# The delta stage in 64-token chunks on strips of the array, and streams' attention values on four strips

## The chip, the cores and the metric

The kernel runs on one core of a Trainium2 chip. The metric is the device time of one execution in microseconds. The engines are TensorE (PE in the profile), VectorE (DVE), ScalarE (ACT), GpSimd (POOL) and SyncE (SP), which here issues most of the loads.

## The reference

One layer of a hybrid streaming encoder: 1024 new tokens of one prompt, and 16 tokens each of 8 running streams (128 tokens), 1152 in all. After a norm and one combined input projection two branches run on the same tokens: attention over a band of 64-token chunks (8 heads of 64), and a gated DeltaNet (4 heads, keys and values of 128). Their outputs are merged by gates, projected, and followed by an MLP. The DeltaNet's part, per head, is this:

```python
q = l2_normalize(qb) * dk ** -0.5; k = l2_normalize(kb)     # qb, kb, vb: causal conv and silu of the projection
g = -exp(a_log) * softplus(a + dt_bias); beta = sigmoid(b)
gc = cumsum(g)                                              # within a chunk of 64 tokens (16 for a stream)
decay = tril(exp(gc[:, None] - gc[None, :]))
A = strict_tril(beta[:, None] * (k @ k.T) * decay) + I
u = solve(A, v * beta[:, None]); w = solve(A, k * (beta * exp(gc))[:, None])
def step(S, chunk):                                         # over the chunks in order
    v_new = u - w @ S
    o = (q * exp(gc)[:, None]) @ S + ((q @ k.T) * decay) @ v_new
    S = S * exp(gc[-1]) + (k * exp(gc[-1] - gc)[:, None]).T @ v_new
ob = rms_norm(o, delta_norm_w) * silu(z)
```

The prompt's state starts at zero, each stream's state is an input, and all final states are outputs.

## The kernel before, in words

The stages run one behind the other: norm, input projection, attention, delta stage, and a tail (projections, merge, MLP). Tokens lie in 9 tiles of 128; tiles 0 to 7 are the prompt, tile 8 holds the streams. Each stage has one program per engine, and engines wait for each other through semaphores.

*Input projection* (stage_in_proj, from L307). TensorE multiplies slabs of weights and tokens; VectorE and ScalarE copy the results out of PSUM. Ahead of the main loop the columns a and b of the gates are made, copied to SBUF (ab_row) and turned by 9 transposes of 8 rows into pab, which VectorE copies to env.ab at L420. Their exp, sigmoid and softplus are worked out later, in the delta stage.

*Attention* (stage_attention, from L510). The work goes in 72 steps, 8 blocks of 8 heads of a prompt tile and one stream: TensorE makes scores (scores_pair L833, scores_stream L844 and L847), VectorE adds the bias and takes the maximum (soft: L718, L721, L737), ScalarE exponentiates (L684), TensorE turns the probabilities (turn, L859) which ScalarE copies (L673), and TensorE makes the values (values_pair L878, values_stream L892). Of each stream all 8 heads stand in the 128 rows of one score tile, 16 rows a head. values_stream multiplies for each of 4 head pairs the transposed values (128 channels of the pair, 5 blocks of keys) by all 128 rows of probabilities: 20 matmuls on the full array, of whose result only a 16-column block per head is used. VectorE picks these blocks with 8 copies of 64x16 (L774). SyncE loads the caches, the relative-position bias (bias_s, 8 loads at L622) and others.

*Delta stage* (stage_delta, from L911). Its order is written out by hand in schedule(): a list of items (kind, tile, step). Every engine walks through that list and does its part of each item (has() says which engine has one), so the list is the order of each engine's queue; wait(engine, item) waits for another engine's part. Tiles are prepared two at a time ("prep": turn, norm_turn, decay, pair, inv0, inv1a to inv5b, solve), with two 64-token chunks side by side in a 128-token tile, block-diagonal, and the four heads in four matmuls of 128x128. In turn q, k and v are transposed into token rows; VectorE makes the normalised and scaled copies, which TensorE turns back in norm_turn and decay. The inverse of the triangular matrix is built over six block sizes (LEVELS 1 to 32): at each, part a multiplies by a masked matrix that GpSimd makes (L1108), ScalarE copies (L1183), part b multiplies twice, and VectorE subtracts twice (L1297, L1299), always 512 columns. Between the preps of a pair stand the "scan" items of the pair before: read (L1454, L1456), then v_new on VectorE (L1307), then write (L1462, L1465), then the state on VectorE (L1310); GpSimd makes the decayed state (L1119). At the end of the list stand the streams' heads (8 masked matmuls with 8 states, each head) and all finals (norm, gate and transposes of the outputs). At its start the stage works out the gates on ScalarE and VectorE, loads the conv output of all tokens in three loads (C, L1051) and takes the row norms of q and k through squares (L1138), pick matmuls (L1354) and transposes (L1359); the gates' z are loaded late.

## Time and profile before

| | us |
|---|---|
| median of 3 runs | 2310.87 (2308.77 to 2315.36) |
| the profiled execution | 2308.39 |
| its span | 2306.7 |
| norm | 0 to 47.3 |
| input projection | 47.3 to 617.0 |
| attention | 617.0 to 884.1 |
| delta stage | 884.1 to 1264.3 |
| tail | 1264.3 to 2306.7 |

Over the span TensorE is busy for 2117.7 us (92%) with 12384 instructions, VectorE for 888.0, ScalarE for 644.4, GpSimd for 610.4. Half of TensorE's time belongs to the input projection and the tail. A share of busy time is an average over stages with different limits; the views by stage and by stretch, the timeline and the durations of single instructions say more for a change within one stage. PEld in the profile is the loading of weights, which runs beside PE. "Clock" is the granted TensorE clock as a share of full speed.

### The profile page before, as it was taken

To read this page: it belongs to the slowest core of one execution; us is meant where nothing else is said; L and a number is where in the kernel's file an instruction comes from. 1 tells how busy PE (TensorE), PEld (TensorE's weight loads), DVE (VectorE), ACT (ScalarE), POOL (GpSimd) and SP (SyncE) were. 2 spreads that over 40 slices of the span, in tenths; PEclk is the share of its full clock that TensorE was granted. 3 is DMA by queue.
4 is the path that set the end of the run, shared out by engine and by line. 5 is a ranking of instruction groups with operands and counts; after the bars stand their busy time and mean duration, and the time that the engine had idled before them with its cause. 6 is when DMAs were issued, how large, how long until landed. Compare 5 with 4: busy or idle time off the path is not lost. (4 is left out here: it accounts for less than half of the span.)

```text
span 2306.7 us, 30588 instructions
## 1 busy us (share of the span) xinstructions
PE 2117.7 (92%) x12384; PEld 1910.0 (83%) x12384; DVE 888.0 (38%) x1600; ACT 644.4 (28%) x1090; POOL 610.4 (26%) x427
## 2 busy tenths in 40 slices
PE   4999999999977777999985999999999999999996
PEld 3999999999855554788874997889999889999884
DVE  3111774111267773444535532822222222222226
ACT  4001221000144444322222532432222222222212
POOL 8121121221000000333312542343233223332314
PEclk7999999999969998999998999999999999999998
DMA  4122225322242203000031532311111111111122
GB/s 123 58 97 77 86 89 218 97 88 86 93 145 74 74 19 124 1 1 1 1 96 55 170 122 89 119 56 46 46 47 37 46 37 37 55 39 45 46 110 83
DMA packets 147001, 168.96 MB, mean 73 GB/s; under 512 B 13707, under 2 KB 115739, under 8 KB 146894
## 3 DMA queue, kind: packets, MB, share of 16 engines
q1 hardware_dynamic: 140558, 141.52, 19.6%
q10 hardware_dynamic: 6336, 25.96, 2.8%
q8 instruction: 74, 1.21, 0.2%
q14 instruction: 33, 0.27, 0.0%
HBM read 126.84 MB, written 40.55 MB: 73 GB/s over the span
## 5 line engine op out<-in xcount | busy, mean ns | idle before, releaser
L2012 DVE TENSOR_TENSOR t_acc<-t_acc,t_B 128x512 f32<-128x512 f32 x270 | 185.1, 687 | 536.3 <-PE t_B L2110 536.2
L116 PE MATMUL i_ps<-x_hi,i_w_lo 128*128 128x384 f32 x1056 | 352.9, 334 | 0.0
L116 PE MATMUL i_ps<-x_lo,i_w_hi 128*128 128x384 f32 x1056 | 352.8, 334 | 0.0
L116 PE MATMUL i_ps<-x_hi,i_w_hi 128*128 128x384 f32 x1056 | 352.8, 334 | 0.0
L2090 PE MATMUL t_B<-t_merged_hi,t_wm_lo 128*128 128x384 f32 x768 | 257.0, 335 | 1.0 <-POOL t_wm_lo L1722 1.0
L2090 PE MATMUL t_B<-t_merged_lo,t_wm_hi 128*128 128x384 f32 x768 | 256.7, 334 | 0.0
L2090 PE MATMUL t_B<-t_merged_hi,t_wm_hi 128*128 128x384 f32 x768 | 256.7, 334 | 0.0
L106 POOL TENSOR_TENSOR i_w_lo<-i_w_raw,i_w_hi 128x1024 fp32r<-128x1024 f32 x44 | 104.9, 2385 | 440.7 <-ACT i_w_hi L101 440.7
L1722 POOL TENSOR_TENSOR t_wm_lo<-t_raw,t_wm_hi 128x1024 fp32r<-128x1024 f32 x48 | 116.5, 2426 | 319.3 <-ACT t_wm_hi L1794 319.3
L116 PEld LDWEIGHTS i_ps<-x_hi,i_w_lo 128*128 128x128 f32 x1056 | 198.2, 188 | 0.0
L116 PEld LDWEIGHTS i_ps<-x_lo,i_w_hi 128*128 128x128 f32 x1056 | 198.2, 188 | 0.0
L116 PEld LDWEIGHTS i_ps<-x_hi,i_w_hi 128*128 128x128 f32 x1056 | 198.2, 188 | 0.0
L429 DVE COPY i_out<-i_ps 128x384 f32<-128x384 f32 x96 | 53.5, 558 | 338.3 <-PE i_ps L116 333.7
L1389 PE MATMUL d_B<-d_pair 128*128 128x128 f32 x1176 | 146.4, 280 | 19.1 <-DVE d_pair L1299 12.1
L1389 PEld LDWEIGHTS d_B<-d_pair 128*128 128x128 f32 x1176 | 137.8, 193 | 29.0 <-issue 21.0
L1756 POOL TENSOR_TENSOR t_f_lo<-t_f,t_f_hi 128x384 fp32r<-128x384 f32 x96 | 97.4, 1016 | 215.2 <-ACT t_f_hi L1893 215.2
L101 ACT ACTIVATE i_w_hi<-i_w_raw 128x1024 fp32r<-128x1024 f32 x44 | 46.6, 1060 | 370.0 <-PE i_ps L116 369.9
L2090 PEld LDWEIGHTS t_B<-t_merged_hi,t_wm_lo 128*128 128x128 f32 x768 | 144.2, 188 | 1.8 <-POOL t_wm_lo L1722 1.3
L1794 ACT ACTIVATE t_wm_hi<-t_raw 128x1024 fp32r<-128x1024 f32 x48 | 50.4, 1051 | 339.9 <-PE t_B L2110 338.1
L2090 PEld LDWEIGHTS t_B<-t_merged_lo,t_wm_hi 128*128 128x128 f32 x768 | 144.2, 188 | 0.6
L2090 PEld LDWEIGHTS t_B<-t_merged_hi,t_wm_hi 128*128 128x128 f32 x768 | 144.2, 188 | 0.0
L2110 PE MATMUL t_B<-t_wm_hi,t_f_lo 128*128 128x512 f32 x288 | 115.1, 400 | 6.5 <-POOL t_lo L1722 5.9
(309 smaller groups left out, 3805.5 us busy)
## 6 DMA issues: line engine op xcount, KB each, us to landing
proj<-i_out ACTq DMA_DIRECT2D x44, 576.0 KB, 2.8
i_w_raw<-in_w_in SPq DMA_DIRECT2D x44, 512.0 KB, 3.9
t_raw<-in_w_up SPq DMA_DIRECT2D x32, 512.0 KB, 4.1
t_raw<-in_w_down SPq DMA_DIRECT2D x32, 512.0 KB, 3.5
d_c<-proj SPq DMA_DIRECT2D x4, 2304.0 KB, 8.6
t_gates<-proj SPq DMA_DIRECT2D x48, 192.0 KB, 2.6
a_k_cache<-in_cache_attn_k SPq DMA_DIRECT2D x8, 1024.0 KB, 6.0
a_v_cache<-in_cache_attn_v SPq DMA_DIRECT2D x8, 1024.0 KB, 5.4
```

The costliest lines, as they stand in the source:

```text
L101: act.activation(w.hi[s][:, :, :], w.raw[s][:, :, :], ACT.Copy).then_inc(w.hi_made, 1)
L106: pool.tensor_tensor(w.lo[s][:, :, :], w.raw[s][:, :, :], w.hi[s][:, :, :].bitcast(F32), ALU.subtract).then_inc(w.lo_made, 1)
L116: last = pe.matmul(out, a[s][:, c, :], b[:, c, tokens], start=k == 0, stop=k == n - 1)
L429: dve.tensor_copy(st[s][:, g * TG:(g + 1) * TG], ps[3 * s + g][:, 0:TG]).then_inc(free, 1)
L1389: last = pe.matmul(bank[:, h, :], a, r, start=True, stop=True)
L1722: pool.tensor_tensor(flat(lo), flat(raw[n % 2]), flat(h).bitcast(F32), ALU.subtract).then_inc(lo_made, 1)
L1756: pool.tensor_tensor(f_lo[j % 2][a][:, group(g)], f[e % 2][:, :], f_hi[j % 2][a][:, group(g)].bitcast(F32), ALU.subtract).then_inc(f_lo_ma ...
L1794: act.activation(flat(made_in(key)[0]), flat(raw[n % 2]), ACT.Copy).then_inc(hi_made, 1)
L2012: dve.tensor_tensor(a, a, B[(ND * j + d) % 4][:, :], ALU.add).then_inc(added, 1)
L2090: last = pe.matmul(B[5 + e % 3][:, 0:TG], p_[:, cc, :], q_[:, cc, group(g)], start=n == 0, stop=n == 3 * DC - 1)
L2110: last = pe.matmul(B[(ND * j + d) % 4][:, :], p_[:, tile(t)], q_[:, cols], start=n == 0, stop=n == 5)
```

## The change

In the delta stage a unit of work is now a chunk of 64 tokens instead of a tile of 128; there are 18, the two of the streams first (chunks 0 and 1), in groups of four (GROUPS; the last has two). The four heads h = 2p + x lie as pairs: x chooses the partitions 0 to 63 or 64 to 127, p the columns. A matrix of 64x64 per head thus takes a 128x128 operand (128 partitions, 2 x 64 columns), and a matmul of a head works on a strip or on a quarter of the array: reads of keys (128 rows) on two column strips, the levels on two quarters.

q and k are not normalised first: pair takes raw k against raw k and q, and multiplies by the decay on the way out (one VectorE instruction); the scales 1/|k|^2, |k| and 1/|q| enter as a column per token at the scaled identity s0 (GpSimd), the factor of x0, the copy of v, and the final norm (bq). The decay is a matmul of a strictly-after matrix with cumulated gates, and one exp on ScalarE per group. Row norms are made per group: two squares on ScalarE ("sums"), pick matmuls on four strips, a copy to rows, then 2 small matmuls a chunk ("cols") that bring them to tokens.

The streams' heads run as chunks 0 and 1 in group 1, on masked copies by GpSimd (item "mask"), with the states loaded at the start of the stage. The finals of a group are two groups behind its prep. The gates (softplus, exp, sigmoid) are worked out in the input projection, behind its 36 small matmuls that take the place of the 9 transposes, and the conv outputs of the first group are loaded in the attention, on SyncE ahead of the bias_s loads. Small constants are picked by GpSimd in the attention, which has no other work there.

In the attention values_stream multiplies, for each head pair j, the 32 rows of probabilities of that pair as weights by the 128 value channels: 20 matmuls on four column strips, rows 32j to 32j+31 of one 128x128 result. VectorE copies it once; a new job X of TensorE turns it some steps later, in the next block, and ScalarE copies two halves to their place.

The diff, cut to its core:

```diff
 # stage_norm_in: GpSimd
-                pool.tensor_scalar(env.shut[:, k, :], env.cum[:, k, :], -NEG, NEG, ALU.mult, ALU.add).then_inc(const, 1)
 # stage_in_proj
+            act.activation(env.beta[:, :, :], env.ab[:, :, 1, :], ACT.Sigmoid).then_inc(gact, 1)
+            act.activation(env.alog[:, :], env.alog[:, :], ACT.Exp).then_inc(gact, 1)
...
-            for t in range(NT):
-                last = pe.transpose(pab[:, t, :], ab_row[:, t * P:(t + 1) * P], env.ident[0:2 * HB, 0:2 * HB])
+            for n in range(2 * NT):
+                for x in range(2):
+                    last = pe.matmul(pab[64 * x:64 * x + 64, n, :], ab_row[:, first:first + 64],
+                                     env.ident[0:2 * HB, 0:2 * HB], start=True, stop=True)
 # stage_attention
+            for a, ts in ((0, TP), (P, 0)):
+                sp.dma_start(env.c0[:, :, a:a + P], env.proj[...]).then_inc(env.c_in, 16)
...
-                    for j in range(4):
-                        for half in range(2):
-                            ins = dve.tensor_copy(env.oa[...], O[u % 2][64 * half:64 * half + 64, col:col + TS])
+                    dve.tensor_copy(so[:, :], O[u % 2][:, 0:P]).then_inc(av_read, 1)
...
+                elif kind == "X":
+                    last = pe.transpose(TR[:, 0:P], so[:, :], env.ident[:, :])
...
-                        last = pe.matmul(O[u % 2][:, j * P:(j + 1) * P], vals, pt[u % 2][:, i * P:(i + 1) * P],
+                        last = pe.matmul(O[u % 2][rows, 0:P], pt[u % 2][:, i * P + 2 * TS * j:i * P + 2 * TS * (j + 1)],
+                                         vals, start=i == 0, stop=i == 4)
 # stage_delta: the order
+    def steps(n):
+        return (["pair", "turn", "x0", "x0t"] + [f"{j}{x}" for j in range(1, levels(n)) for x in "ab"]
+                + (["solve"] if n % 2 else []))
+        out = [("grp", 0, "decay"), ("grp", 0, "sums")]
+        for g, mine in enumerate(GROUPS):
+            other = []
+            if g == 1:
+                other += [("heads", 0, "mask"), ("heads", 0, "read"), ("heads", 0, "out")]
+                for k in range(4):
+                    other += [("heads", k, "spread"), ("heads", k, "write")]
+            if g:
+                other += scans(g - 1)
+            if g + 1 < NG:
+                other.insert(min(3, len(other)), ("grp", g + 1, "decay"))
+            if g >= 2:
+                other += finals(g - 2)
+            per = -(-len(other) // (len(STEPS) - 1))
+            for k, s in enumerate(STEPS):
+                out += [("prep", n, s) for n in mine if s in steps(n)]
+                if s == "pair":
+                    out.append(("grp", g, "cols"))
+                for _ in range(per):
+                    if other:
+                        out.append(other.pop(0))
+            out += other
+            if g + 1 < NG:
+                out.append(("grp", g + 1, "sums"))
+        return out + finals(NG - 2) + scans(NG - 1) + finals(NG - 1)
 # stage_delta: GpSimd
+                elif s == "pair":
+                    pool.tensor_tensor(M[k][:, 0:2, :, :], bc(K, 1, 2), bc(env.levc[:, 0:2, :], 2, 2), ALU.mult)
+                    pool.tensor_tensor(M[k][:, 2:nl, :, :], bc(K, 1, nl - 2), bc(env.levc[:, 2:nl, :], 2, 2), ALU.mult)
+                    ins = pool.tensor_tensor(QK[n % 8][:, :, :], KQ[k][:, :, 0, :], ..., ALU.mult)
+                elif s == "turn":
+                    ins = pool.tensor_tensor(S0[k][:, :, :], bc(env.identc[:, :], 1, 2), bc(s_[:, n, :], 2, L), ALU.mult)
 # stage_delta: TensorE
+                        for x, p in XP:                     # pair: raw k against k and q
+                            ins = pe.matmul(b[half(x), 2 * L * p:2 * L * p + 2 * L], Cn[:, 4 + h, tok(n)], Cn[:, h:h + 5:4, tok(n)], ...)
+                        for x, p in XP:                     # x0; the levels have the same form
+                            ins = pe.matmul(b[half(x), p * L:p * L + L], M[k][half(x), 0, p, :], S0[k][half(x), p, :], ...)
+                            for x, p in XP:                 # solve, for U
+                                ins = pe.matmul(B[km][half(x), 256 + p * P:256 + p * P + P], DD[km][half(x), 1, p, :], U0[km][half(x), p, :], ...)
+                        for x, p in XP:                     # scan, read
+                            pe.matmul(Z0[half(x), p * P:p * P + P], W_of(n, x, p), S[:, x, p, :], start=True, stop=True)
```

## Rows read from the trace of the kernel before

**Rows 1.** Stages (start:end length, busy PE, PEld, DVE, ACT, POOL, clock, DMA, GB/s)

```profile
47.30:617.00 569.70, 565.38 (x3249) 556.71 (x3249) 168.22 (x282) 76.24 (x69) 105.22 (x45) 0.99 0.29 96
617.00:884.10 267.10, 203.82 (x1628) 150.42 (x1628) 184.58 (x545) 118.32 (x244) 0.00 (x0) 0.90 0.24 80
884.10:1264.30 380.20, 319.75 (x2311) 273.85 (x2311) 174.63 (x277) 108.24 (x190) 109.08 (x89) 0.95 0.13 40
```

**Rows 2.** Times of three stretches of the delta stage: start, steady, close

```profile
884.10:913.50 29.40, 20.14 (x67) 7.27 (x67) 3.42 (x12) 16.70 (x21) 2.70 (x5) 0.83 0.67 241
1017.00:1068.00 51.00, 46.93 (x367) 41.88 (x366) 25.74 (x40) 15.36 (x32) 18.43 (x15) 1.00 0.00 1
1208.00:1264.30 56.30, 35.63 (x223) 28.04 (x222) 31.43 (x49) 11.97 (x12) 15.43 (x10) 0.89 0.15 42
```

**Rows 3.** Timeline of the delta stage (start, length, ..., [idle before <-releaser]); L1389's group

```profile
1005.29 0.68 DVE L1299 TENSOR_TENSOR d_pair<-d_pair,d_B 128x512 f32<-128x512 f32 x1
1006.11 1.13 PE L1389 MATMUL d_B<-d_pair 128*128 128x128 f32 x8 [0.58 <-DVE d_pair L1299]
1008.10 1.04 PE L1456 MATMUL d_Z<-d_state,d_quad 128*64 128x128 f32 x8
1009.06 4.73 PE L1389 MATMUL d_B<-d_pair 128*128 128x128 f32 x40
1009.17 0.68 DVE L1307 TENSOR_TENSOR d_v_new<-d_quad,d_Z 64x512 f32<-64x512 f32 x1 [3.20 <-PE d_Z L1456]
...
L1389 PE MATMUL d_B<-d_pair 128*128 128x128 f32 x1176 | 146.4, 280 | 19.1 <-DVE d_pair L1299 12.1
```

**Rows 4.** Timeline of the attention, TensorE: matmuls on two and on four column strips

```profile
758.40 1.31 PE L878 MATMUL a_O<-a_p_t,a_v_tok 128*64 128x128 f32 x20 [1.62 <-DVE oa_ob L774]
767.17 1.07 PE L844 MATMUL a_S<-a_k_cache_t,a_q_diag 128*32 128x512 f32 x8 [0.33 <-DVE a_q_diag L789]
768.03 0.43 PE L847 MATMUL a_S<-k,a_q_diag 128*32 128x128 f32 x8
```

**Rows 5.** Timeline of the delta stage: eight-row transposes

```profile
912.88 0.72 PE L1359 MATMUL d_Z<-ident,d_quad 8*128 8x8 f32 x9 [1.57 <-DVE d_quad L1231]
```

**Rows 6.** Durations by engine: timelines, then lines of instructions (ns min/median/max)

```profile
754.76 0.41 DVE L721 SCALAR_TENSOR_TENSOR a_s<-a_S,a_bias 128x256 f32<-128x256 f32 x1
...
905.61 1.16 ACT L1138 ACTIVATE d_pair<-d_c 128x1152 f32<-128x1152 f32 x1 [0.77 <-PE d_B L1354]
906.79 1.28 ACT L1157 ACT_TABLE_LOAD   x1
915.77 1.14 ACT L1171 ACTIVATE d_quad<-d_B,d_vec 128x128 f32<-128x128 f32 x4 [1.80 <-PE d_B L1387]
...
1001.88 1.04 POOL L1119 TENSOR_TENSOR d_state_decayed<-d_state,d_g_last 128x512 f32<-128x512 f32 x1 [1.63 <-DVE d_state L1310]
1007.32 1.27 POOL L1108 TENSOR_TENSOR d_pair<-d_pair,level 128x512 f32<-128x512 f32 x1 [0.43 <-PE d_B L1389]
...
L1100 POOL TENSOR_TENSOR d_pair<-d_pair,level x9: 1264/1717/1722, 932.1 to 1181.5; 128x512 f32<-128x512 f32 x9
...
L1128 POOL TENSOR_TENSOR d_c<-d_c,d_g_last x4: 1911/1912/1913, 1220.2 to 1243.9; 128x1024 f32<-128x1024 f32 x4
```

**Rows 7.** Timeline of the attention around a stream's values; then its waits

```profile
748.29 1.06 PE L892 MATMUL a_O<-a_p_t,a_v_cache 128*128 128x128 f32 x8
...
754.23 0.62 DVE L718 TENSOR_SCALAR a_s<-a_S,a_bias 128x384 f32<-128x384 f32 x1 [3.53 <-PE a_S L833]
756.79 1.46 DVE L774 COPY oa_ob<-a_O 64x16 f32<-64x16 f32 x8
...
DVE a_s L718 <- PE a_S L833: 32.3, 13, 6.8
```

**Rows 8.** Timeline of the attention: loads of the streams' bias and their first reader

```profile
634.45 5.04 SPq L622 DMA_DIRECT2D a_bias_s<-a_bias  x8
...
650.41 0.23 DVE L736 COPY a_bias_own<-a_bias_s 128x128 f32<-128x128 f32 x1 [1.80 <-PE a_S L847]
```

More of the change, by code:

```diff
@@ L588, in jobs @@
             b, h = divmod(st, STEP)
+            if b and h == AH - 3:
+                out.append(("X", stream(b - 1)))
             if b < NB and h in (AH - 4, AH - 2):
@@ new lines, in stage_delta, with first_token, levels @@
+    NC = NT * 2
+    SAMPLE = 2
+    GROUPS = [range(a, min(a + 4, NC)) for a in range(0, NC, 4)]
+    NG = len(GROUPS)
+    def first_token(n):
+        return TP + L * n if n < SAMPLE else L * (n - SAMPLE)
+    def levels(n):
+        return 4 if n < SAMPLE else len(LEVELS)
+    def steps(n):
+        return (["pair", "turn", "x0", "x0t"] + [f"{j}{x}" for j in range(1, levels(n)) for x in "ab"]
+                + (["solve"] if n % 2 else []))
+    STEPS = ["pair", "turn", "x0", "x0t"] + [f"{j}{x}" for j in range(1, len(LEVELS)) for x in "ab"] + ["solve"]
@@ new lines, in scans, with finals @@
+    def scans(g):
+        return [("scan", n, x) for n in GROUPS[g] if n >= SAMPLE for x in ("read", "write", "out")]
+    def finals(g):
+        return [("fin", g, x) for x in ["mean", "norm"] + [f"turn{i}" for i in range(len(GROUPS[g]) // 2)]]
+    def schedule():
+        out = [("grp", 0, "decay"), ("grp", 0, "sums")]
[23 more added lines that the diff above has]
+        return out + finals(NG - 2) + scans(NG - 1) + finals(NG - 1)
@@ L950, in stage_delta @@
     SCHED = schedule()
     def has(eng, item):
-        kind, t, *rest = item
+        kind, n, s = item
+        if kind == "grp":
+            return {"decay": ("pool", "pe", "act"), "sums": ("act", "pe", "dve"), "cols": ("pe", "act", "dve")}[s].count(eng)
         if kind == "prep":
-            s = rest[0]
-            lev = int(s[3]) if s.startswith("inv") else None
-            return {"pe": True,
-                    "act": s in ("turn", "norm_turn", "decay", "solve") or s.endswith("a"),
-                    "dve": s in ("turn", "norm_turn", "decay", "pair", "inv0") or s.endswith("b"),
-                    "pool": s in ("norm_turn", "pair", "inv0") or (s.endswith("a") and lev + 1 < levels(t))}[eng]
@@ L961, in has @@
[L961 to L967 removed]
+            return {"pair": ("pe", "dve", "pool"), "turn": ("pe", "act", "dve", "pool"), "x0": ("pe", "dve"),
+                    "x0t": ("pe", "act"), "solve": ("pe", "act")}.get(
+                        s, ("pe", "act") if s.endswith("a") else ("pe", "dve")).count(eng)
@@ L969, in stage_delta @@
+        if kind == "scan":
+            return {"read": ("pe", "dve", "act", "pool"), "write": ("pe", "dve"), "out": ("pe", "dve", "act")}[s].count(eng)
+        if kind == "heads":
+            return {"mask": ("pool",), "read": ("pe", "dve", "act", "pool"), "out": ("pe", "dve", "act"),
+                    "spread": ("dve",), "write": ("pe", "dve")}[s].count(eng)
+        return {"mean": ("dve", "act"), "norm": ("dve",)}.get(s, ("pe", "dve")).count(eng)
     place = {}
     for eng in ("pe", "act", "dve", "pool"):
-        for kind in ("prep", "scan", "heads"):
-            for n, item in enumerate(x for x in SCHED if x[0] == kind and has(eng, x)):
-                place[(eng, *item)] = n + 1
+        for kind in ("grp", "prep", "scan", "heads", "fin"):
+            for i, item in enumerate(x for x in SCHED if x[0] == kind and has(eng, x)
+                                     and not (eng == "act" and x[2] in ("sums", "out"))):
+                place[(eng, *item)] = i + 1
@@ L1037, in stage_delta, with at @@
-        rows = [B[0][i][0:2 * HB, :, :].rearrange("p a b -> p (a b)")[:, 0:TG] for i in range(NTG)]
-        block = c.enter_context(nc.Block())
-        def kb_of(t):
-            return 0 if t < NPT else 1
-        def squares(dve, item):
-            wait(dve, "act", *item)
-            dve.tensor_reduce(sso[:, item[1], :], sqo[:, :, :], AX.X, ALU.add).then_inc(dstep, 1)
+        def at(name, shape, offset):
+            return nc.alloc_sbuf_tensor_at("d_" + name, shape, F32, offset=offset)
```

1075 lines of the change are left out of this document (612 added, 463 removed).

## The prediction

> **What bounds the kernel now.** I read the times by stage first [rows 1]. PE is busy for 565 of the 570 us of the input projection, for 204 of the 267 us of the attention, and for 320 of the 380 us of the delta stage. The tail behind them is not touched. The share of busy time of the whole span (PE 92%) therefore says little about a change to the delta stage: the stage has its own limits. Cut into three [rows 2], it has a start of 29.4 us in which PE mostly waits for loads and the gates' arithmetic, a steady part (51 us for one pair of 128-token tiles, PE busy 46.9, VectorE 25.7, ScalarE 15.4, GpSimd 18.4), and a close of 56.3 us with the running streams' states, PE busy 35.6. In the steady part PE's own stream is the bound: 0.92 of the time, at full clock.
>
> Next I read the spacing of PE's instructions [rows 3]. Each fp32 matmul leaves two records. Forty records of the full array with 128 moving columns span 4.73 us; one lasts 0.28, so they start (4.73 - 0.28) / 39 = 0.114 apart, and the eight of 1008.10 by the same working (1.04 - 0.28) / 7 = 0.109. I use 0.112. The stage has 2311 records [rows 1]; at about 0.112 to 0.14 (some move 512 columns) they are its 320 us. On strips the same columns cost less [rows 4]: twenty records of 128 columns on two column strips take 1.31 us and start (1.31 - 0.28) / 19 = 0.054 apart, I use 0.055; eight of 512 columns on four strips take 1.07, against 8 x 0.45 if they ran one after the other at the full array's rate.
>
> **Delta stage, the sum of PE's work.** A 64-token chunk now issues, in records: pair 8, turn 16, x0 8, x0t 8, levels 4 x 24 + 16 = 112, solve 16, scan read 16, write 8, out 8; 200 in all. Of these 64 move 128 columns on two strips (0.055, so 3.5 us) and 136 move 64 columns. The trace has no such record. Half the columns on two halves of the array that work together is 0.027; from above, nine eight-column transposes span 0.72, at most 0.08 each [rows 5], though they move next to nothing: there every record loads a full width of weights by itself. Half of 0.112, 0.055, is a 64-column record that shares the array with nothing. I take 0.027, since the strips' rows, with loads of their own on each strip, are the nearest, and keep 0.055 as the other end: 136 x 0.027 = 3.7 us. A chunk is then 7.2 us, a group of four 28.8, and with decay (one matmul of 512 columns, 2 x 0.43), sums (16 records of 256 columns on four strips, 0.85), cols (16 small ones, 0.43) and the last transposes (8 of 0.112, 0.9) it is 31.8. Two tiles of 128 tokens had PE busy for 46.9 [rows 2]; the same 256 tokens are now 31.8.
>
> Changes of shape come on top. From the first of the eight records of 1008.10 to the next form at 1009.06 [rows 3] lie 0.96 us, so 0.96 - 7 x 0.109 = 0.20 from the last of them instead of 0.11: 0.09 more. Some 26 changes in a group are 2.3 us. The Trainium skill (TensorEngine Tiling (Array Packing), Tiling Modes, Key Properties) says that a change of tiling mode drains TensorE. A whole drain would be about the 0.28 that one record lasts, an estimate, and would add 26 x (0.28 - 0.09) = 4.9 us to a group, some 15 to 20 to the stage; the row of the change with 0.09 speaks for less, though it is a change between forms of full height and no row shows one between halves and quarters.
>
> **Delta stage, the waits.** The engines beside PE, per group, by [rows 6]: VectorE about 25 us (a 256-column combine is 0.41), ScalarE about 28 (128-column copies 0.29, two squares of 1024 columns at about 1.05, which is 1.16 by columns, three table loads of 1.28), GpSimd about 16 (1.27 for 512 columns of two operands, 1.04 with a scalar spread over them, up to 1.72 while VectorE works beside it). The mean of a part that no row shows is taken by its columns. None is above PE's 31.8, but all are close, so the order of the waits sets the time. One step of a level is: PE's last record to its reader 0.31 (in [rows 3] the last of eight starts at about 1008.86, VectorE at 1009.17), a copy 0.29 (a quarter of ScalarE's 1.14, [rows 6]), 0.14 back to PE (1005.97 to 1006.11), then the same with 0.41; 1.6 us of latency and 0.65 of PE for one chunk. Four chunks go round in turn and offer 2.6 us of PE per level, so a level covers itself. What does not cover itself, in a steady group:
> - x0 waits for GpSimd. Its queue holds four masks first (256 columns 0.6, 512 columns 1.27, 128 columns 0.38, so 2.25 each, 9.0 in all, from 1.2 on), then the decay of the state 1.04, and only then the scaled identities that x0 needs, at 11.8 us; PE has 8.5 of work until then. 3.3 us; at the 1.72 of the slow masks the 9.0 are 12.2 and the wait 6.5.
> - The group's end. "sums" needs two squares on ScalarE, queued behind the copies of the solve step; "cols" follows behind a VectorE copy. 4.5 us.
> - The scan's v_new goes PE, VectorE, PE: 0.9 twice where nothing else is queued, 1.8 us.
> - The last norm switches ScalarE between sqrt, silu and exp: 3.9 us of ScalarE, of which 2.5 reach PE.
>
> Together 12, so a steady group is 31.8 + 2.3 + 12 = 46, and two of them 92. The start: the conv columns are loaded during the attention, and the gates are made in the input projection, so what took 29.4 takes about 8.5. The first group has no scan: 4 x (7.2 - 32 x 0.055) = 22, with 3 for decay, sums and changes and 8 of the waits 33. Group 1 carries the streams' states: GpSimd makes eight masked copies (its read waits until 12.6), then scales the states by their decay (4 x 1.91 = 7.6 [rows 6]), and only then reaches the scaled identities, so x0 starts at 24.6; four spreads and writes in a chain cost about 3.5 each, of which a scan's work hides most. 46, 12.8 for the later x0 and 2 for the chain: 61 us. Group 4 has two chunks to prepare (11) and four scans (7), with 2 for the rest and 8 of waits: 28. After it come the finals of group 3, four scans, each a closed chain of read, v_new, write, state, and the last finals: 19.5. The sum is 8.5 + 33 + 61 + 92 + 28 + 19.5 = 242. The granted clock was 0.95 over the stage before [rows 1] and fell where PE had waited; with more waits I add 8. **Delta stage 250 instead of 380: -130.**
>
> **Attention.** A stream's values were 20 matmuls, 40 records on the full array, eight in 1.06 us [rows 7], 4.5 us in all. Now they run on four strips of 32 columns; at 0.028 a record 1.2 us, 3.3 less. Behind them VectorE waits for the next scores (3.53 us ahead of 754.23; 32.3 us in 13 such waits in the stage), so nearly all of it is on the path, 6 x 3.3; a granted clock of 0.90 over the stage [rows 1] means that about a fifth of it ran at the lower level, and I count two of the eight streams there, 6.5 each. The eight small copies (1.46) become one of about 0.3, -1.17 each, on VectorE, which is the busier engine here (185 of 267 us). The added transposition and its two copies cost about 0.5 on PE and ScalarE in each of eight streams. 20 + 13 + 9 - 4 = 38; some of it is hidden where PE and VectorE take turns: **-34**, between -28 and -38. The two loads of conv columns (786 KB each) go on SP ahead of the eight bias loads [rows 8], which are issued from 634.45 to 639.5, with their first reader at 650.41; 0 to 2 us, taken at 0. GpSimd's picks run while it has no other work there [rows 1], at nothing; ten small operations; without that cover they are about 5 us, at the 0.5 that half of 1.04 gives.
>
> **Input projection and norm.** 9 transposes (0.72, [rows 5]) become 36 matmuls, 72 records with 64 weight columns: 72 x 0.07 = 5.0, half of it if strips work together, so +1.8 to +4.5, taken +2.5. The gates' ten small operations stand ahead of VectorE's copies of the results; PE has six banks of slack before it would wait. Ahead of that waits ScalarE's sigmoid and exp with their table loads; its next work is due later than they end. Two GpSimd operations leave the norm, together 0.7 at half of GpSimd's 1.27 each or somewhat less: -0.7, or nothing if GpSimd isn't last there.
>
> **Sum.** The profiled execution is 2308.4 (span 2306.7 and 1.7 around it), the median 2310.9, 2.5 above. 2308.4 - 130 - 34 + 2 = 2146, and on the median's scale **2149**.
>
> **The rivals.**
> - B: 64-column records cost 0.055, since strips don't overlap in loads. For it: the eight-column transposes. Against it: the 0.054 of two strips in [rows 4], where loads of 64 columns overlap. 4 x 136 x 0.028 = 15.2 more per group, about two thirds of it not under the waits: stage 290, time 2190. Chance 0.2.
> - C: the waits overlap better, a steady group is 37 and group 1 45. For it: the sums of every engine are below 32. Stage 200, time 2099. Chance 0.2.
> - E: PE waits so often that the clock is granted at half through much of the stage, as in the pieces of 0.83 to 0.89 [rows 2]. Stage 330 or more, time 2230 to 2280. Chance 0.06.
> - D, slower: matmuls on quarters (64 rows by 64 columns) do not run together, and each record costs the 0.112 of a full one. That is 152 of a chunk's 200 records: 152 x 0.112 + 48 x 0.055 = 19.7 us, a group 84, the stage 425, the time 2324. The stage may grow by 34 - 2 = 32 us, to 412, before the kernel is slower, and that is reached at 0.107 a record; [rows 4] and the halved columns speak against it, though no row shows a quarter at work. Chance 0.04.
> - The change does not do what it says, in that latency holds the stage at its old length: about 2300 to 2312. Chance 0.03.
>
> **How the numbers follow.** My own case, 2149, has 0.47. The range of 2088 to 2212 takes in B and C and the bounds on the attention (10 us), the clock (8) and the drain (15), and leaves E, D and the last out with tails of the first three, some 0.2. Within 0.3% (7 us, about what a measurement of this kernel can tell) lies only part of the last case: 0.02. Slower: D and its neighbours, 0.04. Faster: 0.94.
>
> **What the profile would show.** The delta stage some 250 us long with PE busy for about half to two thirds of it; starts of 64-column records 0.027 apart within a step (0.055 or more would be B, 0.11 D); PE's largest waits named after GpSimd's scaled identity at x0, after ScalarE's squares at "sums", and after the streams' decay in group 1; values of a stream in 1.2 us and VectorE's wait for the next scores gone; the input projection longer by 2 to 3 us. The forecast is wrong if a steady group is far from 46 us, or if the stage's granted clock falls under 0.8.

## The result, and the profile after

The changed kernel takes 2215.6 us (2211.1 to 2220.8), the kernel before on the same chip 2311.5. The ratio is 0.9594, with a 95% interval of 0.9578 to 0.961: 4.1% faster. The forecast was 2149 with a range of 2088 to 2212: the sign was right, the size was not. Of the 162 us that were forecast 96 came.

The stages of the changed kernel, in the view by stretches:

```profile
core 0: us, PE busy (x) PEld busy (x) DVE busy (x) ACT busy (x) POOL busy (x), PEclk, DMA share, GB/s
46.40:621.60 575.20, 569.02 (x3312) 561.06 (x3312) 169.44 (x289) 80.94 (x76) 105.15 (x45) 0.99 0.29 96
621.60:854.55 232.95, 174.80 (x1636) 118.39 (x1636) 175.48 (x489) 122.71 (x260) 2.81 (x10) 0.92 0.29 97
854.55:1167.35 312.80, 219.50 (x3810) 179.83 (x3810) 115.48 (x304) 121.44 (x354) 82.46 (x110) 0.81 0.15 45
1167.35:2209.40 1042.05, 1012.82 (x5112) 915.52 (x5112) 340.28 (x459) 316.36 (x540) 353.58 (x217) 0.99 0.22 69
```

Before, the attention's first instruction stands at 619.0, two us behind the cut of [rows 1]; with that cut the stages of before are 571.6, 265.2 and 380.1 us. By the column of TensorE the input projection and the tail are 569 and 1013 of its 1993 us: four fifths of its time, and three quarters before (1577 of 2118), not the half that was given for the kernel before.

| stage, us | before | forecast | after |
|---|---|---|---|
| norm | 47.4 | -0.7 | 46.4 |
| input projection | 571.6 | +2.5 | 575.2 (+3.6) |
| attention | 265.2 | -34 | 232.95 (-32.3) |
| delta stage | 380.1 | -130 | 312.8 (-67.3) |
| tail | 1042.4 | 0 | 1042.05 |

Everything but the delta stage came about as forecast. There 63 us are missing. Its seven parts (start; groups 0 to 4, each cut where its row norms or its last preparation end; the close) in the same view:

```profile
854.55:861.90 7.35, 3.45 (x18) 2.42 (x19) 0.47 (x4) 1.98 (x5) 3.44 (x5) 0.62 0.86 262
861.90:905.80 43.90, 32.60 (x610) 26.75 (x611) 13.81 (x38) 17.03 (x46) 10.65 (x17) 0.79 0.21 54
905.80:981.20 75.40, 50.95 (x934) 39.60 (x938) 26.83 (x65) 22.64 (x74) 23.19 (x31) 0.82 0.21 64
981.20:1040.40 59.20, 44.36 (x843) 37.88 (x843) 24.35 (x65) 26.79 (x78) 15.86 (x21) 0.88 0.12 38
1040.40:1098.30 57.90, 44.90 (x846) 38.41 (x848) 23.79 (x65) 27.10 (x79) 15.42 (x21) 0.85 0.09 25
1098.30:1139.60 41.30, 32.29 (x496) 26.87 (x496) 18.05 (x48) 14.95 (x50) 10.55 (x13) 0.79 0.05 15
1139.60:1167.35 27.75, 10.94 (x82) 7.90 (x78) 8.19 (x19) 10.96 (x22) 3.34 (x2) 0.62 0.06 19
```

The forecast had 8.5, 33, 61, 46, 46, 28 and 19.5, and 8 for the clock over all of them. Every part but the start is 8 to 14 us longer; no single place holds the loss. In the steady groups (981.2 and 1040.4) TensorE is busy for 44 and 45 of 59 and 58 us, and VectorE, ScalarE and GpSimd for 24, 27 and 16: the sums forecast for the three (25, 28, 16) hold, and none of them is the bound. The clock, the column behind GpSimd's, is 0.81 over the stage, against 0.95 before [rows 1].

What TensorE waits for in the delta stage, by the waits (us in total, times, longest):

```profile
PE d_B L1702 <- DVE d_o L1524: 25.2, 5, 6.7
PE d_B L1558 <- POOL d_g_cum L1227: 19.6, 5, 6.6
PE d_B L1564 <- ACT d_sq L1314: 15.9, 10, 2.2
PE d_B L1675 <- POOL d_q_masked L1271: 9.4, 1, 9.4
PE d_B L1656 <- DVE d_v_new L1475: 8.3, 11, 2.1
```

In order: the finals' transpositions behind the norm, the next group's decay behind GpSimd, the row norms behind ScalarE's squares, the streams' heads behind GpSimd's masked copies, the scan's write behind v_new. They are 78 us together. Where they stand in one steady group, by the timeline of all engines:

```profile
981.15 0.64 PE L1564 MATMUL d_B<-d_sq,pick 128*32 128x256 f32 x8 [2.22 <-ACT d_sq L1314]
983.02 1.08 PE L1564 MATMUL d_B<-d_sq,pick 128*32 128x256 f32 x8 [1.23 <-ACT d_sq L1314]
...
990.38 0.72 PE L1656 MATMUL d_B<-d_v_new,d_kd 64*128 64x128 f32 x8 [2.06 <-DVE d_v_new L1475]
...
996.03 1.46 POOL L1252 TENSOR_TENSOR d_s<-identc,d_vec 128x128 f32<-128x128 f32 x4
997.45 1.03 POOL L1227 TENSOR_TENSOR d_g_cum<-cumc,g 128x512 f32<-128x512 f32 x1
998.63 1.10 PE L1558 MATMUL d_B<-d_g_cum,after 128*128 128x512 f32 x2 [3.31 <-POOL d_g_cum L1227]
...
1016.50 1.28 ACT L1380 ACT_TABLE_LOAD   x1
1018.00 1.28 ACT L1382 ACT_TABLE_LOAD   x1
1020.62 1.23 DVE L1524 TENSOR_TENSOR d_o<-d_o,d_vec 128x1024 f32<-128x1024 f32 x1
1022.00 1.09 PE L1702 MATMUL d_B<-ident,d_o 128*128 128x128 f32 x4 [4.85 <-DVE d_o L1524]
1023.01 1.98 PE L1613 MATMUL d_B<-d_dd,d_m 64*64 64x64 f32 x32
```

At the group's start TensorE stands 2.2 us for the first square and 1.2 for the second. At 990.38 the write stands 2.1 for v_new, which comes on VectorE behind the five operations of the column scales (987.75 to 990.0). GpSimd makes the masks of four chunks and a decayed state, then from 996.03 the identities, and only then the operand of the decay, which TensorE meets at 998.63. At 1016.50 ScalarE loads the table for the roots, then the one for silu, and only when both are done does VectorE norm and TensorE turn: 4.9 us of standing. By the code the norm needs the roots alone, which are done at 1018.00; but VectorE waits for the item's end, behind the silu, and starts at 1020.39. In the close the same costs 2.4 and 2.0 us again; no run tests a wait for the roots alone. The last line is the price that comes behind: 32 records that take 1.15 us at full clock (1013.70, below) take 1.98.

To see how much of a group is which, I took the starts of all matmul records and cut each gap into four: the spacing that its form (rows and columns of the array, columns moved) has at full clock; up to 0.15 us more where the next record belongs to another line of the kernel; a second spacing where the granted clock was at its lower level, 1.2 GHz; and what is left, the wait.

| group 2, us | forecast | measured |
|---|---|---|
| records | 31.8 | 33.3 |
| changes of form | 2.3 (26 of 0.09) | 5.2 (43 changes of line, 29 of them with other rows or columns) |
| waits | 12 | 15.3, and 2.4 in small pieces |
| half clock | (8 for the stage) | 3.1 |
| sum | 46 | 59.3 |

Over the whole stage the same working gives 154 us for records, 26 for 201 changes of line, 116 for waits and small pieces, and 20 for the clock; it ends at the tail's first matmul, some 3 us behind the stage. The forecast's terms for the stage are about 143 (18 chunks of 7.2 and 3 more a group), 10, 89 and 8. So the miss is +11, +16, +27 and +12: spread over every term, and all of one sign. Two of the terms are less sharp than that. Only 131 of the 201 are changes of rows or columns, which is what the forecast counted; at some 0.14 each they are 18 us, and the rest of the 26 is small pieces at other changes of line. And where a gap holds both a wait and half clock, their shares hang on the order in which they are taken off: taken off by runs of eight records, the clock is some 32 us instead of 20 and the waits as much less. So a price for the clock has to come from a run (e4_filler).

The prices of the records themselves, by TensorE's timeline: first part b of a level, then a change of line on quarters, then the solve step:

```profile
1009.47 0.40 PE L1621 MATMUL d_B<-d_x,d_dd 64*64 64x64 f32 x8
1009.70 0.40 PE L1621 MATMUL d_B<-d_dd,d_x 64*64 64x64 f32 x8
...
1013.70 1.15 PE L1613 MATMUL d_B<-d_dd,d_m 64*64 64x64 f32 x32
1014.68 0.61 PE L1661 MATMUL d_B<-d_v_new,d_qk 64*64 64x128 f32 x8
1015.12 0.40 PE L1621 MATMUL d_B<-d_x,d_dd 64*64 64x64 f32 x8
...
974.16 0.66 PE L1630 MATMUL d_B<-d_dd,d_kbe 64*128 64x64 f32 x8
974.75 0.65 PE L1633 MATMUL d_B<-d_u,d_dd 64*64 64x128 f32 x8
975.33 0.66 PE L1630 MATMUL d_B<-d_dd,d_kbe 64*128 64x64 f32 x8
```

Eight records on quarters take 0.23 us from run to run, 0.029 each, against the 0.027 of the forecast. A change of line that stays on quarters costs next to nothing: 32 records and the change behind them take 0.98, 0.05 more than 32 spacings of 0.029. In the solve step a run of eight and the change behind it take 0.59, for the 64-column records on row strips as for the 128-column ones on quarters.

In the attention a stream's values and what follows (timeline, then VectorE's wait for the next scores):

```profile
737.21 1.08 PE L952 MATMUL a_O<-a_v_cache,a_p_t 128*32 128x128 f32 x32
738.11 0.40 PE L952 MATMUL a_O<-a_v_tok,a_p_t 128*32 128x128 f32 x8
742.38 0.28 DVE L833 COPY a_stream_out<-a_O 128x128 f32<-128x128 f32 x1
...
DVE a_s L779 <- PE a_S L889: 15.4, 12, 3.2
```

40 records take about 1.3 us instead of 4.5 [rows 7], one copy of 0.28 stands where eight of 1.46 stood, and the wait for scores fell from 32.3 us to 15.4.

### The profile page after: what moved, and what is told of

Same layout as the page of the kernel before. It is cut to its first block and busy times, and to the rows that moved or that the text cites. A ratio compares the mean times of both kernels' runs of the same rounds, so it can differ in the third digit from the quotient of the medians.

```text
span 2209.4 us, 34183 instructions
## 1 busy us (share of the span) xinstructions
PE 1993.2 (90%) x13954; PEld 1788.8 (81%) x13954; DVE 821.3 (37%) x1578; ACT 666.7 (30%) x1277; POOL 585.9 (27%) x456
## 5 line engine op out<-in xcount | busy, mean ns | idle before, releaser
L2319 PE MATMUL t_B<-t_hi,t_f_lo 128*128 128x512 f32 x288 | 114.6, 398 | 0.0
L2319 PE MATMUL t_B<-t_wm_hi,t_f_hi 128*128 128x512 f32 x288 | 113.7, 395 | 0.0
```

The lines of the kernel that those rows point to most:

```text
L2319: last = pe.matmul(B[(ND * j + d) % 4][:, :], p_[:, tile(t)], q_[:, cols], start=n == 0, stop=n == 5)
```

## The experiments

Theory W says that the delta stage is long because TensorE, which walks through its list in order, stands in line behind chains on other engines; another order of the same list must give most of it back. Rival C says that the granted clock is the price (it is near the prediction's E, and not the prediction's C). Rivals M and G say that ScalarE's table loads or GpSimd's sum of work hold TensorE in any order.

Each stage length below comes from one profiled execution. The four executions of the changed kernel lie between 2211.1 and 2220.8 us, and the profiled one is the shortest; so a few us between two stages, as in e2_fin_late and e8_solve_grouped, are no result by themselves.

**The attention alone (e1_att_only).** The kernel before with three edits of the attention: values on four strips, the copy, the job X.

```diff
-                        last = pe.matmul(O[u % 2][:, j * P:(j + 1) * P], vals, pt[u % 2][:, i * P:(i + 1) * P],
+                        last = pe.matmul(O[u % 2][rows, 0:P], pt[u % 2][:, i * P + 2 * TS * j:i * P + 2 * TS * (j + 1)], vals,
```

> The kernel before with the attention's part of the change alone: values of a stream on four strips, one copy, the later transposition; delta stage, gates and loads as before. If the attention's gain is this alone and the stages add up, the attention takes about 233 us instead of 265 as in the changed kernel, the delta stage stays at 380, and the kernel takes 2311 - 32 = 2279 us. If instead part of the 32 us belongs to something else of the change (clock left by the input projection, loads), it gains less than 25.

Measured: 2280.9 us, ratio 0.9877 (0.986 to 0.9893). Attention and delta stage:

```profile
619.95:852.75 232.80, 173.62 (x1636) 116.77 (x1636) 175.48 (x489) 122.69 (x260) 0.00 (x0) 0.93 0.27 90
852.75:1236.30 383.55, 322.76 (x2311) 275.41 (x2311) 174.46 (x277) 108.51 (x190) 109.21 (x89) 0.94 0.13 40
```

The attention takes 232.8, as in the changed kernel: its 32 us belong to these edits alone. The whole gained 27 instead of 32, since the delta stage, which is the old one, took 383.6 at a clock of 0.94 instead of 380.1 at 0.95; the start and the place of the half-clock stretches differ from run to run by such amounts.

**The finals' transpositions later (e2_fin_late).**

```diff
-                other += finals(g - 2)
+                other += finals(g - 2) if g == NG - 1 else finals(g - 2)[:2]
...
+                if 2 <= g < NG - 1 and s in ("4b", "5b"):
+                    out.append(finals(g - 2)[2 + (s == "5b")])
```

> The changed kernel with the finals' two transpositions moved in the hand-written order from the middle of groups 2 and 3 to behind the levels' parts 4b and 5b, where the norm is long done. Theory W (the delta stage is long because TensorE stands in line behind chains on other engines): the waits of 4.9 us ahead of them in groups 2 and 3 go, the delta stage falls from 313 by 8 to 12 us. Rival C (the low granted clock is the price, and a wait is only where it shows): the waits go but the stage falls by less than 4. Rival M (ScalarE's two table loads hold up the level's copies wherever TensorE stands): a wait of 2 to 4 us reappears at the level's part b behind them, and the stage falls by 2 to 6.

Measured: 2213.3 us, ratio 0.9579 (0.9555 to 0.9602). The delta stage, and TensorE's wait for a level's copy in groups 2 and 3:

```profile
857.40:1168.35 310.95, 221.64 (x3810) 182.29 (x3810) 114.87 (x304) 120.60 (x354) 82.45 (x110) 0.81 0.16 45
...
PE d_B L1623 <- ACT d_x L1352: 5.8, 2, 3.4
```

Group 2 fell by 3.4 us and group 3 by 2.3, from the first pair record to the next group's (59.4 to 56.0, 56.6 to 54.3). The wait of 4.9 became one of up to 3.4 for the copy d_x, which stands on ScalarE behind the same two table loads. That is rival M for this move: the stop is ScalarE's, and moving only its reader moves the wait. The stage fell by 1.9 only, since groups 0 and 1, which the edit doesn't touch, took 6 us more with the clock at half for longer (57 us of the two instead of 44). The 1.9 alone would fit rival C as well; it is the wait at the copy that speaks for M.

**Row norms early (e3_sums_early).** The item "sums" is cut into two squares (q0, q1, ScalarE) and two runs of matmuls (s0, sums).

```diff
+                if g + 1 < NG:
+                    out += [("grp", g + 1, x) for x in {"3a": ("q0",), "4a": ("s0", "q1"), "5a": ("sums",)}.get(s, ())]
             out += other
-            if g + 1 < NG:
-                out.append(("grp", g + 1, "sums"))
```

> The changed kernel with the next group's row norms moved from the group's end into its levels: the first square behind part 3a, its pick matmuls and the second square behind 4a, the second matmuls behind 5a. Theory W: the waits of 2.3 and 1.6 us at the end of groups 0 to 3 go, 4 x 3.9 = 15 us, less about 1 us a group for squares that get in the way of the levels' copies: the stage falls by 9 to 15 us. Rival C: by less than 5.

Measured: 2201.8 us, ratio 0.9542 (0.9526 to 0.9558). The delta stage:

```profile
854.40:1154.25 299.85, 215.47 (x3810) 177.43 (x3810) 116.34 (x304) 121.25 (x354) 82.58 (x110) 0.82 0.16 46
```

13.0 us less, as theory W has it, with the clock at 0.82 instead of 0.81.

**Spare matmuls where TensorE waits (e4_filler).**

```diff
+            def spare(n):
+                for _ in range(n):
+                    pe.matmul(Z7[:, 0:128], env.ident[:, :], env.ident[:, :], start=True, stop=True)
...
+                        if n:
+                            spare((0, 28, 24, 12, 9)[n] if s == "decay" else 8)
...
+                    if i == 0:
+                        spare((20, 20, 12, 24, 24)[n])
```

> The changed kernel with spare matmuls of the full array (results unused) where TensorE waits in the delta stage: ahead of the decay 28, 24, 12 and 9 of them in groups 0 to 3, ahead of the row norms 8, ahead of the finals' transpositions 12 to 24, each shorter than the wait it fills by the profile. Nothing else moves. It shows what the granted clock costs. By the records of the changed kernel at half clock that is 20 us over the stage, and the clock of the stage rises from 0.81 to 0.9 or more: the stage falls by 5 to 15 us. If the clock is not what TensorE's waits bring down, the clock stays and the stage grows by 0 to 10.

Measured: 2197.4 us, ratio 0.9526 (0.951 to 0.9543). The delta stage, and TensorE around the finals of group 2:

```profile
854.70:1148.70 294.00, 241.24 (x4220) 207.01 (x4220) 113.63 (x304) 120.88 (x354) 82.60 (x110) 0.95 0.16 48
...
1014.00 4.73 PE L1540 MATMUL d_B<-ident 128*128 128x128 f32 x40
1019.41 1.15 PE L1619 MATMUL d_B<-d_dd,d_m 64*64 64x64 f32 x32
```

The stage fell by 18.8 us with more work in it (4220 records instead of 3810), and its clock rose from 0.81 to 0.95. Forty spare records stand in the wait of 4.9 us, and the 32 records behind them take 1.15 instead of 1.98. A share of 0.81 over 312.8 us is 2 x 0.19 x 312.8 = 119 us at the half level; 0.95 over 294.0 is 29. So the half level cost this kernel some 19 us by the stage, and some 16 by the ratios of the whole kernel (0.9594 and 0.9526), and it came with TensorE's waits. The result is a little above the expected 5 to 15.

**No roots and no silu (e5_no_tables).** Square in their place, so that ScalarE loads no table; one of the three lines:

```diff
-                    act.activation(rso[:, tiles, :], rso[:, tiles, :], ACT.Sqrt)
+                    act.activation(rso[:, tiles, :], rso[:, tiles, :], ACT.Square)
```

> The changed kernel with square instead of sqrt and silu in the delta stage's groups (the roots of the norms and the gate's silu are left out, the outputs of the DeltaNet branch with them): ScalarE loads no tables there but the first. Four loads of 1.28 us a group go from ScalarE. Theory W (waits): the wait of 4.9 us ahead of the finals' transpositions falls to about 2.4, the one at the end of the last groups likewise, the decay's exp comes 1.3 earlier; the stage falls from 313 by 12 to 20 us, the clock's share with it. If ScalarE's loads were hidden beside other work, by less than 6.

Measured: 2197.1 us, ratio 0.9509 (0.9484 to 0.9535). The delta stage:

```profile
856.55:1152.80 296.25, 217.94 (x3810) 178.56 (x3810) 114.30 (x304) 97.13 (x336) 82.55 (x110) 0.83 0.16 47
```

16.6 us less, within the 12 to 20 of theory W. ScalarE's busy time fell by 24 us, from 121 to 97. The gain stands where the finals stand: 4.6 us in group 2, 4.8 in group 3 and 8.6 behind them, and TensorE's wait for the finals fell from 25.2 to 12.8.

**Heads and decay later (e6_heads_late).**

```diff
-            if g + 1 < NG:
-                other.insert(min(3, len(other)), ("grp", g + 1, "decay"))
+            first = 3 if g == 1 else 0
...
-                for _ in range(per):
+                for _ in range(per if k >= first else 0):
...
+                if s == "1b" and g + 1 < NG:
+                    out.append(("grp", g + 1, "decay"))
```

> The changed kernel with two places of the hand-written order moved: the streams' heads of group 1 begin behind x0t instead of behind pair, and the next group's decay stands behind part 1b instead of ahead of turn. Theory W: TensorE waits 6.5, 5.6, 3.4 and 2.5 us for the decay's operand in GpSimd's queue and 9.5 for the streams' masked copies; half or more of these 27 us come back, since x0 still waits for GpSimd's masks: the stage falls by 10 to 18 us. Rival G (GpSimd's sum of work in group 1, about 30 us of masks, copies and decays, is the bound there): the waits move to x0 and to the heads' write, group 1 keeps its 75 us and the stage falls by less than 6.

Measured: 2194.1 us, ratio 0.9498 (0.9479 to 0.9517). The delta stage:

```profile
854.40:1150.05 295.65, 217.59 (x3810) 180.94 (x3810) 115.32 (x304) 119.87 (x354) 82.93 (x110) 0.83 0.16 47
```

17.2 us less, from the first pair record to the next group's 6.3 in group 0 and 11.6 in group 1, and nothing in groups 2 and 3, where the wait moves from the decay to other places. TensorE's waits for the decay and the masked copies fell from 29 us to 5. GpSimd's work is the same (82.5 us before and 82.9 now): its sum was not the bound, its order was.

**The three moves together (e7_all_late)**, with the transpositions behind 3b and 4a and the row norms' pieces behind 3a (not 3b, as the text below has it), 4b and 5b, since they share a bank; in group 1 the pieces stand behind solve.

> All three moves of the order together: finals' transpositions (behind 3b and 4a), row norms (first square behind 3b, 4b, 5b, in group 1 left at the end), heads and decay late. Theory W: about the sum of the parts, 25 to 40 us less than the changed kernel's 313 in the delta stage, 2180 to 2190 us in all. If the waits only trade places (one chain behind the others), 15 or less.

Measured: 2181.6 us, ratio 0.9442 (0.9423 to 0.9461). The delta stage:

```profile
856.50:1138.35 281.85, 212.48 (x3810) 176.84 (x3810) 115.00 (x304) 118.73 (x354) 82.87 (x110) 0.85 0.17 49
```

31.0 us less, within the expected 25 to 40; the single moves add up to 1.9 + 13.0 + 17.2 = 32.

**Solve by form (e8_solve_grouped).**

```diff
                                 pe.matmul(B[slot(n - 1) + x][:, a:a + L], kbe[km][half(x), p, :], DD[km][half(x), 1, p, :], ...)
-                            for x, p in XP:
+                        for m in (n - 1, n):
+                            km = slot(m)
+                            for x, p in XP:
```

> The changed kernel with the solve step's matmuls grouped by form: for a pair of chunks two runs of row strips, then two of quarters, instead of four changes. It prices a change of form between strips and quarters. By the starts of the changed kernel a run of eight records and the change behind it take 0.59, of which 0.15 is the change; four changes less in a group are 0.6 us, 2 to 3 us in the stage and no more. If a change drained the array for the length of a record (0.27), about 1.0 a group and 4 in the stage.

Measured: 2210.5 us, ratio 0.9567 (0.9542 to 0.9593); by time too near the changed kernel to say more. The solve step by TensorE's timeline:

```profile
1035.73 1.11 PE L1630 MATMUL d_B<-d_dd,d_kbe 64*128 64x64 f32 x16
1036.77 1.09 PE L1635 MATMUL d_B<-d_u,d_dd 64*64 64x128 f32 x16
```

Sixteen records of one form and the change behind them take 1.04 (and 1.02 in the next run) instead of 2 x 0.59 = 1.18: one change less is 0.15 us. From the last record's start to the next form it is 1.04 - 15 x 0.055 = 0.21, less than the 1.11 - 15 x 0.055 = 0.28 that this record lasts in the profile, where the ends of matmuls are modelled. Over the stage that is 4 x 0.15 x 4.5 groups = 2.7 us, as expected; the stage's 308.9, 3.9 below the changed kernel, can't show so little.

**A better order (e9_order), and the same with spare matmuls (e10_order_fill).** The order of e7_all_late with its places shifted by a step or two, the final norm moved away from the roots (they stand behind 2a, the norm behind 3b), solve by form, and the last finals between the last scans. e10_order_fill has spare matmuls besides, and ahead of each batch a wait until the bank that they write is read:

```diff
+            elif g + 1 < NG:
+                at_step = {"3b": sq(g + 1, "q0"), "5a": sq(g + 1, "s0", "q1"), "5b": sq(g + 1, "sums")}
+            if g >= 2:
+                mean, norm, *turns = finals(g - 2)
+                for s, xs in (("2a", [mean]), ("3b", [norm]), ("4a", turns[:1]), ("4b", turns[1:])):
+                    at_step[s] = xs + at_step.get(s, [])
...
+        return out + [mean] + last[:3] + [norm] + turns + last[3:] + finals(NG - 1)
```

> The order of the run with all moves, with three more: the final norm on VectorE stands two steps behind the roots on ScalarE (it held up VectorE's queue, 4.2 us in groups 2 and 3), the solve step is grouped by form, and the last finals are interleaved with the last scans. Theory W: 2 x 3 + 4 + 3 to 6 us less than the 282 of that run in the delta stage, about 268; the kernel at 2167 to 2172. Rival M (ScalarE's loads and roots hold the level's copies in any place): the 4.2 us stay as waits of a level's part, 275 or more.

> The same with spare matmuls (results unused) in six places where TensorE still waits: ahead of x0 in groups 0 and 1 (10, 18), ahead of the decay and the row norms of group 2 (14, 8), ahead of the last two finals' transpositions (8, 20). By the filler run on the changed kernel (19 us for 95 us less at half clock) and with 70 to 100 us at half clock in the version without: 5 to 12 us less than that. If the clock's price was a matter of that kernel's order alone, no gain or a loss of up to 5.

Measured: 2168.7 us, ratio 0.9384 (0.9368 to 0.94), and 2165.9 us, ratio 0.9369 (0.9354 to 0.9385). The delta stage of e9_order and TensorE's largest waits in it, then the delta stage of e10_order_fill:

```profile
858.20:1125.90 267.70, 203.31 (x3810) 169.84 (x3810) 115.49 (x304) 118.49 (x354) 83.05 (x110) 0.88 0.18 52
...
PE d_B L1716 <- DVE d_o L1535: 11.0, 5, 5.7
PE d_B L1670 <- DVE d_v_new L1486: 9.4, 9, 2.5
PE d_B L1633 <- ACT d_x L1361: 8.9, 7, 2.4
PE d_B L1611 <- POOL d_s L1264: 7.4, 2, 4.7
PE d_B L1575 <- ACT d_sq L1326: 7.2, 6, 2.2
```

```profile
854.90:1123.00 268.10, 219.82 (x3966) 186.80 (x3966) 116.48 (x304) 118.00 (x354) 83.11 (x110) 0.92 0.18 52
```

The same work in another order takes 45 us less in the stage, 267.7 as expected; that is 18 above the 250 of the prediction, about what records and changes of form cost more than forecast, which the order leaves as they are. The five largest waits are 44 us instead of 78. The finals' wait fell from 25.2 to 11.0; in the order of its lines these are the finals, v_new, a level's copy, the identities for x0 and the row norms. The copy's wait (8.9) is what is left of rival M. The spare matmuls raised the clock from 0.88 to 0.92 and gave the stage nothing (268.1): by the starts of the records the half level costs 11.9 us without them and 9.6 with them. Of the 22 us at half clock that they took away, 14 lay in group 4 and the close, where TensorE has little to do; that the spare records and their waits delay others is likely, and not shown. The expected 5 to 12 us did not come; the price of the clock depends on where the half level falls. Both kernels beat the changed one by 2%; the few us between the two lie in the attention (236.6 and 233.3), which is the same in both.

## Why the prediction was wrong, step by step

**Right.** The bound of the old stage and the spacing of records: quarters at 0.029 for 0.027, so that rivals B (0.055) and D (0.11) fall. The three engines' sums. The attention (-32 for -34): 3.2 us a stream for the values, 9 us less work on VectorE, and e1_att_only shows that nothing else has a part in it; but the wait for scores, called gone, still has 15.4 of its 32.3 us, and the rest of the sum was not taken apart. The start of the delta stage (7.35 for 8.5), the norm. Three of the four places of waits in a steady group, and the size at the row norms (2.3 + 1.6 and small ones for 4.5, by the starts); the fourth, GpSimd's queue, has its size (3.3 for 3.3) but is met at the decay and not at x0.

**Right in part by luck: the input projection.** Its +3.6 lies within +1.8 to +4.5. The 36 matmuls take 2.8 us (63.06 to 65.85) where the transposes took 0.65 (65.10 to 65.75), +2.1 for the +2.5. The main loop behind them took 2.5 us more, with the clock at half until 71.3, and the part ahead of them 1.0 less, with the clock up 3 us earlier; neither was forecast.

**Wrong: the waits.** 89 us were forecast for the stage, 116 measured, and a steady group was 59 and 58 us instead of 46, the sign of failure that the forecast had named. The finals were put at 2.5 of 3.9 us of ScalarE; all of it and the norm behind it reach TensorE, 4.9, since VectorE's norm waits until both table loads and the silu are done, and TensorE for the norm. In five finals that is 25.2 us, the largest wait of all, where the forecast named GpSimd's identities, the squares and the streams' decay as the largest. v_new was put at 0.9 twice; at 990.38 alone it is 2.1, behind the column scales on VectorE. In group 0 the decay's operand stands in GpSimd's queue behind all four masks, 6.6 us, and in group 1 again 5.6, behind the 9.4 for the heads. The forecast put these on x0 in group 1 and left group 0 with the steady group's waits. It also read four scans into group 1 and into the close, where scans() gives two (the streams' chunks have none, and the last group has two chunks); so the close is 8 us longer than forecast with half of its scans. The step that failed is the reading of schedule(): I asked what each item waits for, but not, at each item of TensorE's list, how long the other engines' queues are at that point. e3_sums_early, e6_heads_late and e9_order show that these waits are the order's and not the work's.

**Wrong: the changes of form.** Their price, more than their number: 26 were counted in a group, there are 29 (131 in the stage), and at full clock each costs 0.12 to 0.15 us where nothing else holds the next record, and 0.24 out of the full array, instead of 0.09. That is some 18 us instead of 10. The row of before that priced them was one between forms of full height; e8_solve_grouped gives 0.15 between strips and quarters. The Trainium skill (TensorEngine Tiling (Array Packing), Tiling Modes, Key Properties) says that a change of mode drains TensorE. Whether the array drains no row shows; the rows of the solve step have 0.20 from the last record's start to the next form (0.15 beyond the spacing), where the record lasts 0.28 by the profile's modelled ends: the price lies between the 0.09 that was taken and the 0.28 that was weighed, which over 4.5 groups would have been 22 us and not the 15 to 20 of the text.

**Wrong: the clock.** 8 us were added for the stage, e4_filler prices it at 16 to 19, and the 0.81 stands just above the 0.8 that the forecast named as a sign of its failure. Rival E had the mechanism, but at 80 us more for the stage; the runs show some 10 more for the clock.

**Wrong: the records.** 11 us: the 2208 records of 64 columns on quarters at 0.029 instead of 0.027 are 4 to 5 of them. The 144 such records of the solve step that load 128 columns of weights on row strips were counted at 0.027 too, but start 0.055 apart (0.59 less the change), 4 more; and write has 0.06. The heads' 160 records were not in the sum, which the two scans too many in group 1 make up in part.

**The range.** It took in B or C, each as one step, and the bounds of attention, clock and drain beside the forecast. It did not take in that the terms of the delta stage err together: more standing means a lower clock (0.95 before, 0.81 after). 63 us too short in a stage of 250 is a quarter; the bounds that stood in the text (3.3 or 6.5 for one wait, 2.3 or 7.2 for the changes, 8 for the clock) are some 44 us when they are added up over 4.5 groups, most of it, and the finals and the heads' waits had no bound. At the other end, rival C's stage of 200 does not follow from its two terms, which give some 216.

## What to carry to other kernels

When a matmul stage's own work becomes cheaper (46.9 us of records to 33.3 for 256 tokens here), its waits don't: walk along the in-order list of the engine that bounds it, item by item, and write down for each the length of the queue ahead of its operand on every other engine; the order of the list was worth 45 us of 313 here, with the same work. Price a term that hangs on another (a clock that falls with waits) together with it, and let the range add such terms up. A table switch on ScalarE belongs where no other engine needs ScalarE for its length, and its reader several items behind it.

## What the runs showed of the hardware

- Matmuls on two diagonal quarters of the array (64 rows by 64 columns each) ran side by side: 0.029 us for a 64-column fp32 record, half of the 0.055 that a 128-column record takes on two column strips.
- A 64-column record on row strips with 128 weight columns costs the same as a 128-column one on quarters, 0.055: fewer moving columns gave nothing there.
- A change of form between row strips and quarters costs 0.15 us beyond a record's spacing; a change of line that stays on quarters 0.05 or less.
- Spare matmuls in the waits raised the stage's granted clock from 0.81 to 0.95 and made it 18.8 us shorter; in a better order the same device raised it from 0.88 to 0.92 and gave nothing.
